# Dot products and gathers of the gates stage shifted, and one load freed of a wait, in a hybrid streaming layer with PEER experts

## The reference

```python
a = jnp.einsum('td,tkd->tk', xt, u).astype(jnp.float32)      # u = u_tab[eidx]
c = (gt * jax.nn.gelu(a, approximate=False)).astype(xt.dtype)
return jnp.einsum('tk,tkd->td', c, vsel)                     # vsel = v_tab[eidx]
```

## Time and profile before

| what | value |
|---|---|
| median of three executions | 4913.26 us |
| the profiled execution's own time | 4915.87 us |
| its span, first to last instruction | 4914.0 us |
| TensorE matmul, weight load busy | 98%, 96% |
| VectorE, GpSimd, ScalarE busy | 66%, 58%, 30% |
| mean granted TensorE clock | 0.993 |
| the gates stage in the trace | about 2929 to 3725 us |

### The profile page before, as it was taken

How to read it: one execution, slowest core, us unless ns; L and a number is a source line. 1 busy time by engine, 2 the same in 40 slices (tenths; PEclk the granted TensorE clock), 3 DMA queues, 4 the chain that set the end, 5 groups by cost and what they waited for, 6 DMA issues and landing times.

```text
span 4914.0 us, 78844 instructions
## 1 busy us (share of the span) xinstructions
PE 4833.8 (98%) x32224; PEld 4723.9 (96%) x32224; DVE 3250.2 (66%) x4242; ACT 1498.2 (30%) x2899; POOL 2845.9 (58%) x1650
## 2 busy tenths in 40 slices
PE   8999999999999999999999999999999999999998
PEld 8999999999998879999999999999999999999998
DVE  5877777773423544217577777667666998888855
ACT  5333333332423432102211226666662000000001
POOL 7200000003333435555277879999997999999986
PEclk9999999999999999999999999999999999999999
DMA  7333333335343536523344448999998888888852
GB/s 271 117 129 128 129 127 127 122 130 149 108 150 128 202 137 220 194 87 128 125 145 141 142 154 322 337 337 337 335 336 298 303 313 307 305 313 305 316 185 105
DMA packets 343207, 1013.06 MB, mean 206 GB/s; under 512 B 39728, under 2 KB 132112, under 8 KB 307232
## 3 DMA queue, kind: packets, MB, share of 16 engines
q1 hardware_dynamic: 165776, 526.23, 31.7%
q0 software_dynamic: 36864, 268.45, 14.6%
q10 hardware_dynamic: 140208, 213.34, 12.2%
HBM read 882.26 MB, written 126.76 MB: 205 GB/s over the span
## 4 chain that ended last, share of the span: by engine, by line
PE 93%; DVE 4%; POOL 1%; DMA 1%; ACT 1%; issue 1%; ACTq 0%; POOLq 0%; DVEq 0%; SPq 0%
PE ps L248 22%; PE ps L252 21%; PE ps L250 21%; PE ps L761 7%; PE ps L762 7%; PE ps L760 7%; PE ps L2823 1%; PE ps L1153 1%; PE ps L1593 1%; PE ps L1170 1%; DMA ex_gate<-gate 0%; POOL w_lo L221 0%; DVE in_sums L681 0%; PE ps L1559 0%; PE ps L2516 0%
## 5 line engine op out<-in xcount | busy, mean ns | idle before, releaser
L218 POOL TENSOR_SCALAR w_hi<-w_raw 128x1024 fp32r<-128x1024 f32 x678 | 778.4, 1148 | 1903.5 <-PE ps L762 1079.7
L221 POOL TENSOR_TENSOR w_lo<-w_raw,w_hi 128x1024 fp32r<-128x1024 f32 x678 | 1711.7, 2525 | 56.6
L248 PE MATMUL ps<-h_hi,w_hi 128*128 128x416 f32 (+1 forms) x3552 | 1051.5, 330 | 1.0 <-ACT later_beside L410 1.0
L252 PE MATMUL ps<-h_hi,w_lo 128*128 128x416 f32 (+1 forms) x3552 | 1034.7, 326 | 0.0
L250 PE MATMUL ps<-h_lo,w_hi 128*128 128x416 f32 (+1 forms) x3552 | 1026.6, 323 | 0.0
L248 PE MATMUL ps<-ex_c_hi,w_hi 128*128 128x416 f32 x2048 | 718.0, 351 | 5.8 <-DVE ex_y L3123 4.0
L252 PE MATMUL ps<-ex_c_hi,w_lo 128*128 128x416 f32 x2048 | 717.3, 350 | 0.0
L250 PE MATMUL ps<-ex_c_lo,w_hi 128*128 128x416 f32 x2048 | 717.3, 350 | 0.0
L248 PEld LDWEIGHTS ps<-h_hi,w_hi 128*128 128x128 f32 x3552 | 623.2, 188 | 8.9 <-issue 4.8
L250 PEld LDWEIGHTS ps<-h_lo,w_hi 128*128 128x128 f32 x3552 | 622.6, 189 | 6.2
L252 PEld LDWEIGHTS ps<-h_hi,w_lo 128*128 128x128 f32 x3552 | 620.0, 188 | 2.5
(11 more groups left out here) (373 smaller groups left out, 9243.1 us busy)
## 6 DMA issues: line engine op xcount, KB each, us to landing
w_raw<-weights SPq DMA_DIRECT2D x906, 512.0 KB, 3.9
up<-up_out ACTq DMA_DIRECT2D x128, 208.0 KB, 6.4
gate<-g_sb_g ACTq DMA_DIRECT2D x13, 2048.0 KB, 13.7
proj<-rows_out ACTq DMA_DIRECT2D x97, 272.0 KB, 3.4
ex_up<-up ACTq DMA_DIRECT2D x16, 832.0 KB, 8.1
ex_gate<-gate ACTq DMA_DIRECT2D x16, 832.0 KB, 17.4
sp_first<-proj ACTq DMA_DIRECT2D x48, 272.0 KB, 3.5
sp_first<-up ACTq DMA_DIRECT2D x15, 832.0 KB, 7.6
```

Of the source, the lines that this page charges most:

```text
L218: pool.tensor_scalar(self.whi[:, to, :], self.raw[:, slot, :], 1.0, 1.0, ALU.mult, ALU.mult).then_inc(self.hi_done, 1)
L221: pool.tensor_tensor(self.wlo[:, to, :], self.raw[:, slot, :], self.whi[:, to, :].bitcast(F32), ALU.subtract).then_inc(self.split_done, 1)
L248: pe.matmul(acc, hi, x, start=first, stop=False)
L252: mm = pe.matmul(acc, lo, x, start=False, stop=last)
```

## The change

Two edits in the gates stage and one in the experts stage.

1. Dot products to a tile: 8 in the first (none after the first group, one instead of two after the fourth), 10 in the next nine, 11 in the last three. The gather of slot s, from the fourth slot on, comes ahead of the first split n with `6 * (s - 1) <= 5 * n`.
2. The load of the second set's terms waits only for the first four up stores of each parity (up blocks 0 to 7; the load reads 4 to 7). The wait for all 128 stands behind it.

```diff
-    DOTS_AFTER = [1, 1, 1, 2, 1, 1, 1, 2]
+    DOTS_AFTER, DOTS_FIRST, DOTS_MORE = [1, 1, 1, 2, 1, 1, 1, 2], [0, 1, 1, 1, 1, 1, 1, 2], [1, 1, 2, 1, 1, 2, 1, 2]
+    dots_after, LAG = [DOTS_FIRST] + [DOTS_AFTER] * (G_TILES - 4) + [DOTS_MORE] * 3, 2
...
-                while s < SLOTS and 6 * (s - GATHERS) <= 5 * n:
+                while s < SLOTS and 6 * (s - GATHERS + (LAG if s >= GATHERS else 0)) <= 5 * n:
...
-                for _ in range(DOTS_AFTER[group % STEPS]):
+                for _ in range(dots_after[group // STEPS][group % STEPS]):
...
                     for parity in range(2):
                         act.wait_ge(sparse.gates_stored[parity], 16 * ((G_TILES + 1 - parity) // 2))
+                        act.wait_ge(up_blocks.stored[parity], 16 * VSET)
+                    load_terms(1)
+                    for parity in range(2):
                         act.wait_ge(up_blocks.stored[parity], 16 * (N_KEYS // 2))
-                    load_terms(1)
```

## The result

| | median, us | lowest to highest | executions |
|---|---|---|---|
| before | 4909.38 | 4908.87 to 4918.78 | 6 |
| changed | 4944.41 | 4934.90 to 4955.38 | 6 |

The ratio is 1.0073, with a 95% interval of 1.0061 to 1.0085: 35 us slower. The forecast was 4942.8. The executions of the changed kernel lie further apart, over 20 us against 10, but with six of each that shows little: 23 later executions of the kernel before reach from 4900.4 to 4920.2.

What follows compares the result with a forecast made beforehand. TensorE, busy 98% of the span, was taken as the bound, so only its waits and low clock could change the time. 34.6 + 10.8 - 10.9 - 5 = +29.5 us gave a median of 4942.8, 8-in-10 range 4921 to 4960.

Steps and rivals of the forecast that it cites:

- The last three tiles: End of gates stage: dot products catch up, gathers do not; four late chains add 34.6 us, plus 10.8 of low clock.
- s127: Gather slot in the last tile: 19.7 us chain from split 151 makes g102's product 14.7 us late.
- s123: Gather slot ahead of split 147: chain from split 146 makes g99's product 10.1 us late.
- s117: Gather slot ahead of split 140: its chain makes g95's product 4.9 us late.
- s112: Gather slot whose dot product stands at g90, 30 us before the similar s117 case: the same 4.9 us late.
- The low clock: TensorE runs slower after each of the four waits in the last tiles: 4 x 2.7 = 10.8 us added.
- The first tile: Gates stage: TensorE's 2.04 and 4.55 us waits and the low clock behind them go; 10.9 us gained.
- The terms' load: Second down set: load issued 6.8 us earlier, VectorE's wait under 3 us, 5 us gained.
- Rival 1: Late gathers are covered, only gains are left: -10.9 - 5.8, 4896.6 us, faster; 5 in 100.
- Rival 2: Only the last tile's two long chains bind, slack meets the others: +14.3 us, 4927.6; 16 in 100.
- Rival 3: Two of four landings take 14.3 us and the first tile gives nothing: +51.4 us, 4964.7; 12 in 100.
- Rival 4: All cancels within 0.2%: short landings, no low clock, full gains: +6.7 us, 4920.0; 6 in 100.

Runs made afterwards that it cites:

- the gates' part alone: Changed kernel with the second set's terms' load put back behind the wait for all stores; 4947.36 us, ratio 1.0072 to before.
- the one without catching up: Changed kernel with 10 instead of 11 dot products in each of the last three tiles; 4896.16 us, ratio 0.9966 to before; run again, 4895.04 us.
- the kernel with the load alone: Kernel before with only the second set's terms loaded ahead of the wait for the last up stores; 4906.98 us against 4909.73, ratio 0.9995.

## Why the prediction was right

**The last three tiles.** The mechanism was the one forecast, by five signs: without the 11th dot product of a tile nothing is lost, with it and gathers that catch up 0.5 us, with early gathers 7.2, with late gathers alone 208, and TensorE waits for nothing but the one-hots. The forecast was 34.6 + 10.8 = 45.4 us. The profiled execution had 27.3 + 11.3 = 38.6, the longest one of the gates' part alone 60.1; by medians, the changed kernel against the one without catching up, it is 49.4, or 48.3 against its first run.

- s127: chain 19.4 against 19.7 forecast, the difference in landing, 8.6 for 8.8. TensorE waited 9.07 and not 14.7, because part of the lateness had already been paid at g101 (3.44) by a chain that I had put down as lying beside. Together with 1.7 of low clock between them that makes 14.2, near the 14.7 forecast.
- s123: split at 3671.84, g99's product at 3690.20, 18.4 us. Again shared: 3.94 at g98, 1.84 at g99. The first of these belongs to s121, whose gather shared its time with a gate store of 2 MB and let its dot product begin 12.5 us later, behind 9.66 us of waiting.
- s117: 3.75 at g95, forecast 4.9.
- s112: I had it at g91, and there are 0.51; the wait of its kind came two groups earlier, 3.54 at g89.

So "5, 5, 10, 15" was wrong as a list of waits, and about right as a sum (with the low clock 45.4, against 38.6 in this profile and 49.4 by medians), since the chains share their lateness rather than each standing before one product. What failed in the small is the step that took four chains as standing apart, with all others beside them.

**The low clock.** Forecast 4 x 2.7 = 10.8, found 11.3 with nine waits, four of them between 3.4 and 4.0 and one of 9.07. The agreement is partly luck: it is five long waits at 2.0 on the mean (1.5 to 2.9), and not four at 2.7. The 0.55 and 0.66 in front of g8 and g9 left the clock at 1.00.

**The first tile.** Forecast 10.9 gained, measured 9.65, and 8.9 to 9.7 in the other kernels that have both parts (against the 120.85 of the kernel with the load alone, whose gates stage is that of the kernel before, it would be 7.7). The rest, 0.55 + 0.66, is two short waits that I had counted as gone.

**Nine tiles.** Forecast nothing, found 542.88 against 542.88 from the third tile to the eleventh.

**The terms' load.** This step failed in its size. I took 5 and said that VectorE's wait would be under 3 us; it is 6.41 (8.55 before), and the gain is about 3. I had let the landing move with the load, and put most of TensorE's 5.8 us of waits down to it, of which only the first 1.85 stood right behind the landing. It moved by 2.2 of 6.5 us: from the load's issue to VectorE's product it is 26.1 us now and 21.8 before. What stands beside it in the profile is other traffic; that this is the cause is argued and not shown by a run of its own. Every kernel with the moved load shows a second wait of VectorE for y, 9.0 to 12.2 us for the two; each of the three without it has one, 8.4, 8.4 and 5.6. The first y addition kept its place, 5.3 us behind the last up store (5.2 before). The Trainium skill, DMA: Bandwidth & Descriptors, section Queues, rings and completion order, has each DMA engine take turns between queues by packets. The late landing is the direction seen, while the first y addition, which I had said it would slow, was not slowed.

**The sum.** -9.65 + 0 + 38.6 - 2.95 = +26.0 in the profiled execution, +35 by medians; forecast +29.5. Each of the three errors went the same way: 4 too little lost in the last tiles of a typical execution, 1.2 too much gained in the first, 2 too much from the terms. They make 7, which the difference of the medians, 35.0 against 29.5, has as 5.5; that only 1.6 of it show in 4944.4 against 4942.8 is luck: the kernel before was 3.9 us faster at the median of six than at that of the three executions I had. Rival 1 (gains only) is what the kernel without catching up does, 4896.16 against 4896.6. That they meet is the same luck: the gain is 13.6 us, or 15.1 in its second run, where rival 1 had 16.7. What holds of it is that the late gathers alone decide between gain and loss. Rival 2 (4927.6) lies below the shortest execution, and the waits at g89 and g95 speak against it too. Rival 3 is out for the first tile's sake, though the longest executions, 46 and 49 us above the median of before, come near its +51. Rival 4 needed the landings of 6.0, and none of 16 was below 7.3; nor was any in the last two tiles of the kernel before below 7.6. What stays open: which chain catches at which group, and what it costs, changes between executions, and two profiles are too few to say why.

## What to carry to other kernels

When a consumer in an in-order queue is moved, look at its distance from its producer, and move both by the same amount: two places for both cost nothing over nine tiles, two places for the gathers alone cost 16 us a tile. If the consumer catches up later, let the producer catch up with it: this cost 0.5 us in the last two tiles instead of 38.6. Where the only slack is between two releases by the same paced engine, sum the chain from the release that starts it (here 19.7 us against 5 of room), and expect late chains to share one lateness: here the sum came out nearer than the single waits. An earlier issue of a load is not an earlier landing while other loads are in flight: here a third of it arrived.

## What the runs showed of the hardware that I had not expected

- A gather of 128 rows of 8 KB beside a 2 MB store let its dot product start 12.5 us after the issue, against a median landing of 8.6 in the same tiles.
- The terms' load, issued 6.5 us earlier beside the loads of y and of the down weights, was usable 2.2 us earlier.
- A wait of 0.55 or 0.66 us leaves TensorE's clock at 1.00; behind 3.4 us and more its next product took 1.46 instead of 0.84 us in several cases (g95, g98, g102) and 0.84 in another (g101), where the low clock came just behind the product (0.76 up to the next wait, 1.7 us lost).
- Unchanged stages took 7.1 us less in one profiled execution than in the other, a fifth of the effect that was measured here.
